# Two-layer streaming encoder: first projections in a new block order, layer norm's steps between their last pieces, the convolution in one piece on VectorE

## The reference, cut to what matters

```python
def mixer_ab(h, k_cache, v_cache, conv_hist, w_in, rel_bias, conv_w, conv_b, ln_g, ln_b, w_out):
    z = h @ w_in                                  # columns: q, k, v (512 each), a, g (512 each)
    q, k, v = z[..., :512], z[..., 512:1024], z[..., 1024:1536]
    pre_glu = z[..., 1536:]
    att = band_attention(q, k, v, rel_bias)       # chunk of 64 frames, this chunk and 8 before; streams: 512 cached + 16
    conv_out, new_hist = conv_module(pre_glu, conv_hist, conv_w, conv_b, ln_g, ln_b)
    return jnp.concatenate([att, conv_out], -1) @ w_out, k, v, new_hist

def conv_module(pre_glu, conv_hist, conv_w, conv_b, ln_g, ln_b):
    a, g = jnp.split(pre_glu, 2, axis=-1)
    u_ext = jnp.concatenate([conv_hist, a * jax.nn.sigmoid(g)], axis=1)
    y = depthwise_conv(u_ext, conv_w) + conv_b    # 31 taps, causal
    return jax.nn.silu(layernorm(y, ln_g, ln_b)), u_ext[:, -30:]
```

## Time and profile before

| | us |
|---|---|
| median of 3 runs | 3093.26 |
| lowest, highest | 3092.72, 3100.05 |
| the profiled execution, its own time | 3096.99 |
| its span in the trace | 3095.3 |
| PE busy | 2911.2 |
| DVE busy | 1439.9 |
| ACT busy | 701.3 |
| POOL busy | 143.0 |

### The profile page before, as it was taken

The page is one execution under the profiler, slowest core; times in us unless marked ns, Lnnn a source line. Parts: engine busy times, 40 slices in busy tenths (PEclk is TensorE's granted clock), DMA queues, the critical chain, the costliest instruction groups (busy, mean ns, idle before and its releaser), DMA issues.

```text
span 3095.3 us, 50807 instructions
## 1 busy us (share of the span) xinstructions
PE 2911.2 (94%) x21228; PEld 2802.1 (91%) x21228; DVE 1439.9 (47%) x2479; ACT 701.3 (23%) x1148; POOL 143.0 (5%) x235
## 2 busy tenths in 40 slices
PE   5999699979999999999799999989799999999996
PEld 5998367969999999999799999989699999999996
DVE  6888576252333333333634445454623333333335
ACT  3111465031111111111322222231221111111111
POOL 4000211010000000000100000000100000000001
PEclk9999699989999999999899999999899999999998
DMA  3111331101111111111111111112111111111111
GB/s 124 42 48 68 95 131 76 48 21 55 42 42 41 42 41 42 41 43 46 75 49 43 43 43 51 57 54 79 36 55 42 41 42 49 47 41 42 41 35 62
DMA packets 51269, 163.50 MB, mean 53 GB/s; under 512 B 8480, under 2 KB 19664, under 8 KB 48512
## 3 DMA queue, kind: packets, MB, share of 16 engines
q1 hardware_dynamic: 46624, 148.98, 13.9%
q10 hardware_dynamic: 3456, 8.91, 0.8%
q0 software_dynamic: 992, 2.62, 0.4%
HBM read 143.15 MB, written 18.92 MB: 52 GB/s over the span
## 4 chain that ended last, share of the span: by engine, by line
PE 87%; DVE 7%; issue 2%; ACT 2%; DMA 1%; POOL 1%; ACTq 0%; DVEq 0%; POOLq 0%; SPq 0%
PE PS L574 19%; PE PS L576 19%; PE PS L575 19%; PE PS L814 6%; PE PS L815 6%; PE PS L816 6%; DVE HF L685 2%; PE PS L1214 1%; PE PS L1483 1%; PE PS L1221 1%; PE PS L1599 1%; PE PS L1600 1%; PE PS L1601 1%; PE PS L1245 1%; DVE HBL L695 1%
## 5 line engine op out<-in xcount | busy, mean ns | idle before, releaser
L574 PE MATMUL PS<-HAH,WH 128*128 128x384 f32 x1776 | 615.5, 347 | 11.3 <-DVE HBL L695 7.4
L575 PE MATMUL PS<-HAL,WH 128*128 128x384 f32 x1776 | 601.0, 338 | 0.0
L576 PE MATMUL PS<-HAH,WL 128*128 128x384 f32 x1776 | 600.3, 338 | 0.0
L576 PE MATMUL PS<-HBH,WL 128*128 128x384 f32 x1776 | 594.5, 335 | 0.0
L574 PE MATMUL PS<-HBH,WH 128*128 128x384 f32 x1776 | 594.3, 335 | 0.0
L575 PE MATMUL PS<-HBL,WH 128*128 128x384 f32 x1776 | 594.3, 335 | 0.0
L562 DVE TENSOR_TENSOR WL<-WR,WH 128x1024 fp32r<-128x1024 f32 x201 | 244.2, 1224 | 566.5 <-ACT WH L557 564.9
L814 PE MATMUL PS<-UH,WH 128*128 128x384 f32 x1056 | 357.4, 338 | 5.2 <-issue 5.0
L574 PEld LDWEIGHTS PS<-HAH,WH 128*128 128x128 f32 x1776 | 338.5, 191 | 24.0 <-issue 12.2
L815 PE MATMUL PS<-UL,WH 128*128 128x384 f32 x1056 | 356.4, 338 | 0.0
L816 PE MATMUL PS<-UH,WL 128*128 128x384 f32 x1056 | 356.3, 337 | 0.0
(11 more groups left out here) (234 smaller groups left out, 2636.1 us busy)
## 6 DMA issues: line engine op xcount, KB each, us to landing
WR<-w_fi_in SPq DMA_DIRECT2D x88, 512.0 KB, 3.5
WR<-w_fo_in SPq DMA_DIRECT2D x44, 512.0 KB, 3.4
WR<-w_c_in SPq DMA_DIRECT2D x32, 512.0 KB, 4.0
WR<-w_ab_in SPq DMA_DIRECT2D x20, 512.0 KB, 3.5
CACHES<-k_cache_in SPq DMA_DIRECT2D x8, 1024.0 KB, 4.8
CACHES<-v_cache_in SPq DMA_DIRECT2D x8, 1024.0 KB, 6.9
X<-x_t_in SPq DMA_DIRECT2D x3, 1536.0 KB, 10.7
x_spill<-X SPq DMA_DIRECT2D x1, 4608.0 KB, 12.3
```

The source lines that it names most:

```text
L574: nc.tensor.matmul(out, wh, hh(k, third(n)), start=(k == 0), stop=False)
L575: nc.tensor.matmul(out, wh, hl(k, third(n)), start=False, stop=False)
L576: mm = nc.tensor.matmul(out, wl, hh(k, third(n)), start=False, stop=(k == KT - 1))
```

## The change

What it does:

1. The 20 blocks run in the order g0 a0 v0 g1 a1 q0 v1 g2 a2 q1 v2 g3 a3 q2 v3 q3 k0 k1 k2 k3, block i from slot i mod 3. All loops over steps are written out. The third transpose of a v block comes after the first piece of the next block.
2. DVE does each gate and then all 31 taps of the block, with the low parts of the weight blocks at fixed taps (`LOWER`). The low parts of blocks 1, 2 and 3 come before the first gate.
3. Layer norm's PE steps stand at piece borders: the sums of `Y` ahead of the last piece of k2 (index 18), then squares, spread and squares ahead of the three pieces of k3 (index 19); the rest behind it. DVE subtracts the mean of each third as its sum is there. The last third is spread into bank 6. ACT's squares and roots stand between its evictions.
4. POOL loads `BT` and `BS` and clears `QBD` before it waits for the gates, and issues the two state outputs as soon as the last gate is done. ACT's squares no longer wait for `s_outc`; DVE does, before attention's memsets. `BT` has a place of its own behind `QBD`, and DVE subtracts its first column before layer norm.
5. In attention, streams follow chunks 1 to 8 in place of 0 to 7, and PE does the first two scores after the second third's scaling (`s_yc` 5), and goes on at `s_yc` 6.

```diff
-        ROUND = PAIRS + 1
+        ORDER = []
+        for c in range(NCK):
+            ORDER += [(c, f, None) for f in range(PAIRS)]
+            if 1 <= c <= NB:
+                ORDER.append((None, None, c - 1))
...
+        AB_M = dict(g=16, a=12, v=8, q=0, k=4)
+        AB_BANK = dict(g=0, a=3, v=0, q=0, k=3)
+        AB_ORDER = [(k, int(j)) for k, j in "g0 a0 v0 g1 a1 q0 v1 g2 a2 q1 v2 g3 a3 q2 v3 q3 k0 k1 k2 k3".split()]
...
-            sp.wait_ge(s_full["v"], N3 * AB)
+            sp.wait_ge(s_full["k"], N3 * AB)
...
             pool.wait_ge(s_rel, 48)
-            pool.wait_ge(s_cv, 2 * CW * AB)
-            pool.wait_ge(s_co, AB)
-            pool.dma_start(cvp_o, CO[:, :, :]).then_inc(s_outc, 16)
-            pool.dma_start(cvs_o, US[:, :, :, NS:HIST + NS]).then_inc(s_outc, 16)
-            pool.wait_ge(s_outc, 32)
-            pool.wait_ge(s_full["vt"], N3 * AB)
...
             pool.memset(QBD[:, :, :], 0.0).then_inc(s_qd, 1)
+            pool.wait_ge(s_got["a"], N3 * AB)
+            pool.wait_ge(s_co, AB)
+            pool.dma_start(cvp_o, CO[:, :, :]).then_inc(s_outc, 16)
+            pool.dma_start(cvs_o, US[:, :, :, NS:HIST + NS]).then_inc(s_outc, 16)
...
+        def ab_pe(pe, T, ready):
+            LN_AT = {(18, 2): sums, (19, 0): squared, (19, 1): spread, (19, 2): squared}
+            before, late = {}, None
+            for i, (name, j) in enumerate(AB_ORDER):
+                bank = AB_BANK[name]
+                have(pe, T, i % 3)
+                for n in range(N3):
+                    if (i, n) in LN_AT:
+                        LN_AT[(i, n)](pe, T)
+                    if i == 0:
+                        ready(n)
+                    if bank in before:
+                        other, k = before[bank]
+                        pe.wait_ge(s_got[other], N3 * k + n + 1)
+                    product(PS[:, bank + n, 0:TH], i % 3, n).then_inc(s_full[name], 1)
+                    if late is not None:
+                        turn(pe, late, N3 - 1)
+                        late = None
+                    if name == "v" and n:
+                        turn(pe, j, n - 1)
+                before[bank] = (name, j)
+                if name == "v":
+                    late = j
+            spread(pe, T)
+            squared(pe, T)
+            spread(pe, T)
...
+        def sums(pe, T):
+            pe.wait_ge(s_got["q"], N3 * AB)
+            pe.wait_ge(s_cv, 2 * CW * AB)
+            for n in range(N3):
+                for j in range(AB):
+                    mm = nc.tensor.matmul(PS[:, n, 0:TH], ones[:, :], Y[:, j, third(n)], start=(j == 0), stop=(j == AB - 1))
+                mm.then_inc(s_ms, 1)
...
+                    if (i, n) in ((18, 1), (19, 0), (19, 2)):
+                        square(act, T)
+                    if (i, n) in ((18, 2), (19, 1)):
+                        root(act, T)
...
-            act.wait_ge(s_outc, 32)
...
+            LOWER = {(0, 2): 4, (0, 9): 5, (0, 17): 6, (0, 26): 7, (1, 1): 8, (1, 7): 9, (1, 16): 10, (1, 24): 11,
+                     (2, 1): 12, (2, 7): 13, (2, 15): 14, (2, 24): 15, (3, 1): 16, (3, 7): 17, (3, 15): 18, (3, 24): 19}
...
+            for i in (1, 2, 3):
+                cut_lo(dve, T, i % 3)
             for j in range(AB):
-                pe.wait_ge(s_cv, 2 * CW * (j + 1))
...
+                gate(j)
+                conv(j)
...
+            dve.wait_ge(s_outc, 32)
             dve.memset(PRE[:, :, CACHE + CHK:5 * P], 0.0).then_inc(s_bias, 1)
...
+            pe.wait_ge(s_yc, 2 * N3 - 1)
             scores(0)
             scores(1)
+            pe.wait_ge(s_yc, 2 * N3)
```

More of the change, by code:

```diff
@@ new lines, in turn, with cast_bank @@
+        def turn(pe, j, n):
+            pe.wait_ge(s_got["v"], N3 * j + n + 1)
+            need(pe, s_got["vt"], N3 * j + (0, -1, 1)[n])
+            for tt in range(TPT):
+                mm = nc.tensor.transpose(PS[:, 6 + n % 2, tile(tt)], EV[:, n, tile(tt)], ident[:, :])
+            mm.then_inc(s_full["vt"], 1)
+        def cast_bank(n):
+            return 6 if n == N3 - 1 else n
+        def sums(pe, T):
[5 more added lines that the diff above has]
+                mm.then_inc(s_ms, 1)
@@ new lines, in squared, with spread @@
+        def squared(pe, T):
+            if T("ln") == 0:
+                pe.wait_ge(s_got["vt"], N3 * AB)
+            n = T("ln")
+            T.add("ps", 1)
+            pe.wait_ge(s_ps, T("ps"))
+            for tt in range(TPT):
+                mm = nc.tensor.matmul(PS[:, 7, 3 * n + tt:3 * n + tt + 1], LSQ[:, 0, tile(tt)], ones[:, 0:1],
+                                      start=True, stop=True)
+            mm.then_inc(s_ms, 1)
+        def spread(pe, T):
+            n = T("ln")
+            T.add("dg")
+            pe.wait_ge(s_dg, T("dg"))
+            nc.tensor.matmul(PS[:, cast_bank(n), 0:TH], ones[:, :], LDG[:, :, :].rearrange("p a b -> p (a b)"),
+                             start=True, stop=True).then_inc(s_rb, 1)
+            T.add("ln")
@@ new lines, in ab_act, with square, root @@
+            root(act, T)
+        def square(act, T):
+            n = T("lsq")
+            act.wait_ge(s_yc, n + 1)
+            if n:
+                act.wait_ge(s_ms, T_MS + N3 + n)
+            act.activation(LSQ[:, :, :], Y[:, :, third(n)], ACT.Square).then_inc(s_sq, 1)
+            T.add("lsq")
+        def root(act, T):
+            n = T("lrt")
+            act.wait_ge(s_ms, T_MS + N3 + n + 1)
+            act.activation(rt[:, 3 * n:3 * n + 3], PS[:, 7, 3 * n:3 * n + 3], ACT.Sqrt,
+                           bias=eps[:, 0:1], scale=1.0 / AW).then_inc(s_rt, 1)
+            T.add("lrt")
@@ new lines, in ln_act, with conv @@
+        def ln_act(act, T):
+            T.add("ms", 2 * N3)
+            for n in range(N3):
+                act.wait_ge(s_yc, N3 + n + 1)
+                for j in range(AB):
+                    y = Y[:, j, third(n)]
+                    ins = act.activation(y, y, ACT.Silu, bias=sm("lb", j), scale=sm("lg", j))
+                ins.then_inc(s_hf, 1)
+                T.add("hf")
+        def ab_dve(dve, T):
+            LOWER = {(0, 2): 4, (0, 9): 5, (0, 17): 6, (0, 26): 7, (1, 1): 8, (1, 7): 9, (1, 16): 10, (1, 24): 11,
+                     (2, 1): 12, (2, 7): 13, (2, 15): 14, (2, 24): 15, (3, 1): 16, (3, 7): 17, (3, 15): 18, (3, 24): 19}
+            def conv(j):
+                for t in range(CW):
+                    if (j, t) in LOWER:
+                        cut_lo(dve, T, LOWER[(j, t)] % 3)
+                    w = sm("cw", j * CW + t)
@@ L1409, in att_dve @@
             for s in range(ITEMS + 4):
[L1410 to L1411 removed]
+                if s < STREAMED and item(s)[1] == 0 and 1 <= item(s)[0] < NB:
+                    queries(item(s)[0])
                 if s < ITEMS:
```

252 lines of the change are left out of this document (78 added, 174 removed).

## The result

| | before | after |
|---|---|---|
| median, us | 3092.99 (3088.26 to 3100.05, 4 runs) | 3059.53 (3056.20 to 3286.76, 4 runs) |
| ratio | | 0.9886 [0.9862, 0.9911] |
| profiled execution, us | 3096.99 | 3059.66 |
| its span, us | 3095.3 | 3057.9 |
| mean granted clock | 0.97 | 0.977 |

The medians are 33.5 us apart, and the ratio is 1.1% less.

What follows compares the result with a forecast made beforehand. PE, busy for 94% of the span, was taken to bound the kernel. A first Exp 26.2 us earlier plus 1.0 from attention's order gave 27.2 us, so 3066 against the median 3093.26; own range 3062 to 3070, wide 3058 to 3074.

Steps and rivals of the forecast that it cites:

- The sums' border: Piece border before k2's third piece, where PE starts layer norm's sums; forecast at 280.7 us.
- The convolution: DVE's gates, taps and low parts, starting at 71.4 us, forecast done at 277, before PE reaches the sums.
- cover: Time between the convolution's forecast end and PE's border at the sums: 3.6 us; beyond it each us costs one.
- a rival: Convolution late: slower transfers at 60 us or more waits for high parts; slip of 3.6 + 7 us, 3073, chance 0.10.
- Layer norm's steps: PE's sums (7.96 us) and three small steps (0.8 each) between pieces, waits covered; first Exp at 323.1, 26.2 earlier.
- the tail: From the last product's end at 307.7 to attention's first Exp: eviction, square, fold, sum, root, Silu, table loads; 15.4 us.
- the state's output: The convolution state's transfer of 13.99 us, forecast hidden under q2 and v3, lying near 228 us.
- DVE's third multiplication: Late by a low part of 1.2 us, but needed only by the last four Silus, 6 us later.
- The rule on the port: POOL's eight query copies in the last convolution might hold DVE for 8 x 0.23 = 1.9 us at most, within 3.6.
- Attention's order: Streams one chunk later: chunk 0 saves 4.4 us, chunk 8 adds 3.4; net -1.0, bounded by -2.3 and +2.1.
- attention gains: PE's clock comes back sooner after a shorter idle stretch and the order nets -2.3; 5 us more, 3061, chance 0.10.
- The sum: Forecast total gain 27.2 us: 26.2 at the first Exp and 1.0 from attention's order.

Runs made afterwards that it cites:

- conv_short: Changed kernel with three extra linked DVE adds ahead of the last five taps of the last convolution; 3063.18 us, ratio 0.9899.
- conv_long: Changed kernel with fourteen extra linked DVE adds ahead of the last five taps of the last convolution; 3071.36 us, ratio 0.9932.
- ln_behind: Changed kernel with all of layer norm's PE and ACT steps moved behind the last product; 3071.19 us, ratio 0.9923.
- output_late: Changed kernel with the convolution state's output issued behind the last tap and ACT's first square waiting for it; 3064.80 us, ratio 0.9901.
- order_old_again: Changed kernel with streams back behind chunks 0 to 7, run a second time; 3066.23 us, ratio 0.9922.
- after_again: The changed kernel run once more, unchanged; 3062.75 us, ratio 0.9898.
- order_new: The kernel before with only the streams moved behind chunks 1 to 8; 3091.08 us, ratio 0.9988.
- split cuts: Changed kernel with HBH and HBL cut from Y in twelve steps instead of three whole thirds; 3055.85 us, and 3055.47 when run again.
- old_split: Changed kernel with HBH and HBL cut in twelve steps and streams back behind chunks 0 to 7; 3063.03 us, ratio 0.9918.
- early: Changed kernel with twelve-step HBH/HBL cuts, layer norm's steps one piece earlier, bias tables behind the first gate and some low parts later; 3052.96 us, ratio 0.9868.
- early_warm: The kernel early plus 4 and 12 matmuls that nobody reads, placed where PE idled; 3053.37 us, ratio 0.9861.

## Why the prediction was right or wrong

*The sums' border.* Forecast 280.7; the chain has 280.53. It lies at 279.9 to 282 in other traces of the same blocks.

*The convolution.* Forecast done at 277 with a cover of 3.6; 276.5 and 4.1. Three errors cancel in it, so that it came out so well is luck. DVE's first tap stood at 73.72, not 71.4, since ACT got the fourth block 2.7 us later than before: the forecast left that at zero in the sum and named it only as a rival. Against it, the first tap of each convolution is a cheaper instruction, 0.81 in place of 1.28, 1.9 us in all that I had counted as full taps, and DVE waited for no high part later, where I had 0.7.

*Layer norm's steps.* Forecast 7.96 for the sums, measured 7.74 in the chain; the small steps 0.72 and 0.81 where I took 0.8; no idle time ahead of them. The last product ends at 307.0 (forecast 307.7), the tail is 15.15 (forecast 15.4), the first Exp at 322.15 (forecast 323.1), and the state's output is issued at 227.80 (forecast 228). This term is right: 27.2 us against 26.2. conv_short, conv_long, ln_behind and output_late bear it out. One reading was off: the last product of before ended at 298.0, where ACT evicts it, and PE turned v until 298.96. No term hangs on it, since the gain is counted at the first Exp. DVE's third multiplication had less to spare than the 6 us given, about 1 by the estimate above.

*The rule on the port.* The forecast weighed whether POOL's eight copies would hold DVE's taps. They fell under the last convolution, and it was POOL that paid. They took 9.81 us in place of 8 x 0.23 = 1.9, the longest 4.21:

```profile
247.91 9.81 POOL L539 COPY QBD<-X 64x64 f32<-64x64 f32 x8 [17.82 <-ACT X L1029]
```

Over DVE's whole convolution (groups, 72 to 278 us) a tap stayed at 1279 ns, as in the earlier trace rows:

```profile
L1105 DVE SCALAR_TENSOR_TENSOR Y<-UP,small,Y 128x1024 f32<-128x1024 f32 x120 | 153.4, 1279 | 0.0
```

In output_late, where the same eight copies start behind the last tap, they took 2.26. The nine taps beside the stretched copies took 1280 ns on the mean. The Trainium skill says in "SBUF — State Buffer", Who interferes with whom, that of a DVE instruction with two SBUF inputs and a GpSimd instruction that reads SBUF the one that is issued second waits. POOL's stretched copies agree with it. A wait of DVE for POOL is not visible in these taps. The term, at most 1.9 us within the cover, was nothing for DVE.

*Attention's order.* This is the step that failed: **-1.0 us, bounded by -2.3 and +2.1**. Its item part was near: the stream leaving chunk 0 gave 4.34 (I took 4.4), the one entering chunk 8 cost 2.90 (I took 3.4), so -1.4. What it left out is the clock. In the old order PE waits 1.3 us for DVE at the second stream, some 7 us after the clock's return (5 in order_old_again), and the clock falls again; with the streams one chunk later it mostly doesn't. Attention took 177.0 on the mean of four traces with the old order and whole cuts, and 173.2 on the mean of seven with the new one (after, after_again, order_new, ln_behind, conv_short, conv_long, output_late). Of these 3.8 us, 1.4 are the items in chunks 0 and 8 and 2.4 are chunks 1 and 2; the rest of attention is the same on the mean. With split cuts it is 170.8 against 166.6. So the term is -4, outside my bounds: I bounded the work moved and held the clock around it fixed. In the profiled pair it was even -6.0, with 1.6 of scatter at the cuts.

The rival "attention gains", with 0.10, was the one that came in, at nearly its price (5 us more, 3061), but not for its reason. The clock came back no sooner, 12 us behind the first Exp in both before and after (18 in after_again); what went was a second fall.

*The sum.* 27.2 + 3.8 is 31.0. The ratio gives 35 with an interval of 27 to 43, after_again 32. In the profiled pair, whose spans are 37.4 apart, 27.2 lie ahead of the first Exp, 6.0 in attention and 4.2 behind its last item. The last is within what this program scatters by: there all these kernels execute the same instructions, and that part took from 2559.6 us (after_again) to 2570.7 (output_late) in the traces. A median of four to six runs of it cannot tell 3 us.

## What to carry to other kernels

Bounding a moved piece of work by its own duration on both sides is not enough where PE's clock has just changed level: ask what PE waits for in the next 20 us of either order, and put a term for a second fall into the sum (here 1.4 to 3.7 us in the five traces of the old order, over the 19.6 that chunks 1 and 2 take without one). For a transfer or a chain that becomes a condition of PE, work out its cover, add a late start at full price, and test it by adding work just below and just above it. Large steps of helpers (here three cuts of a third) that make PE wait 1 to 2 us are worth splitting even where PE is at full clock, since the wait may also cost the clock: it took 6.6 us off attention in the traces, of which the ratios show 2 to 4.

## What the runs showed of the hardware

The granted clock fell at the second stream, at a wait of PE of 1.31 or 1.32 us, in all five traces of the old order (the fifth is old_split), and in one of eleven of the new, where the wait is 1.21 or 1.22. What PE did before it differs in two ways. In the old order PE idled 1.8 us of the last four, in the new one 1.4 (windows of 1 us, the last being the one in which the transposes start). And in the old order the clock had come back from half 5 to 7 us before those transposes. In the new order it had been back for 12 us and more in seven traces, none of which fell, and for only 6 to 7 us in four (after_again, conv_long, early, early_warm), of which early fell. So the order and the time since the clock's return are not fully parted by these runs. At the cuts, a wait of 2.15 us was followed by 0.55 in after_again and by nothing in after. Why one execution falls and another doesn't was not settled.

The Trainium skill gives in "ScalarE: Activation LUTs", What ACT_TABLE_LOAD costs, about 2.66 us for a switch of tables, about half of it a drain. Here the load alone shows: 1.28 us at 312.26 and at 320.86, with the root ending at 312.24 and the first Silu starting at 313.55. A drain is not visible in this trace.
